# Two latent projections and a gate projection moved ahead of transpositions, and split projections that start on the high halves of their weights

## The reference

```
h = x @ w_in                       # split into a_q a_k a_v a_z | b_cq b_ckv b_kr b_z | c_q c_k c_v c_z
ya = moba_attention(a_q, a_k, a_v) * silu(a_z)      # with 256 tokens: causal softmax with ALiBi, 8 heads
cq, ckv = rmsnorm(b_cq), rmsnorm(b_ckv)             # the latents, up-projected for 8 heads
yb = mla_attention(cq @ w_uq, ckv @ w_ukv, rope) * silu(b_z)
yc = rmsnorm(diff_attention(c_q, c_k, c_v)) * silu(c_z)   # difference of two softmaxes, 4 heads
g  = sigmoid(x @ w_m + b_m)
out = (ga * (ya @ w_a) + gb * (yb @ w_b) + gc * (yc @ w_c)) @ w_o
r = ALPHA * x + out
r = r + sigmoid(r @ w_pg) * (p @ w_p)
return layernorm(r)
```

## Time and profile before

| | us |
|---|---|
| runs: median of 3 (lowest to highest) | 2129.71 (2129.71 to 2130.98) |
| the profiled execution | 2128.94 |
| its span | 2127.1 |
| PE busy | 2095.6 (99%) |
| DVE, ACT, POOL busy | 1412.5, 1297.7, 653.9 |

### The profile page before, as it was taken

One profiled execution on the slowest core, in us unless ns is written; L12 is line 12 of the kernel. 1 busy time (PEld: TensorE's weight loads), 2 busy tenths in 40 slices (PEclk: granted clock), 3 DMA queues, 4 the chain that ended last, 5 costly groups with the idle time before them and its releaser, 6 DMA issues.

```text
span 2127.1 us, 33542 instructions
## 1 busy us (share of the span) xinstructions
PE 2095.6 (99%) x13315; PEld 1865.4 (88%) x13315; DVE 1412.5 (66%) x1431; ACT 1297.7 (61%) x1427; POOL 653.9 (31%) x316
## 2 busy tenths in 40 slices
PE   9999999999999999999999999999999999999998
PEld 8979999988999898999998888888888888888887
DVE  1455223345422684323777989999999999999997
ACT  4556445455544544444545777777777777777776
POOL 5726885726787203888201000000000000000000
PEclk9999999999999999999999999999999999999999
DMA  7434564625455334556447999999999999999995
GB/s 245 137 111 150 176 196 149 189 70 164 151 194 179 121 100 149 191 194 197 141 140 230 382 377 332 376 357 366 363 351 371 362 369 346 364 356 370 367 365 202
DMA packets 307633, 529.06 MB, mean 249 GB/s; under 512 B 11842, under 2 KB 152802, under 8 KB 307520
## 3 DMA queue, kind: packets, MB, share of 16 engines
q1 hardware_dynamic: 306496, 525.92, 70.9%
q0 software_dynamic: 736, 1.00, 0.2%
q10 hardware_dynamic: 288, 0.52, 0.1%
HBM read 525.84 MB, written 1.05 MB: 248 GB/s over the span
## 4 chain that ended last, share of the span: by engine, by line
PE 84%; POOL 7%; DVE 3%; ACT 3%; issue 2%; DMA 1%; POOLq 0%; SPq 0%; DVEq 0%; ACTq 0%
PE bank L718 82%; POOL weights_low L3020 7%; PE bank L1474 1%; DVE qb L2288 1%; ACT sc L1619 1%; DMA ring<-in_w_in_dram 1%; ACT weights_high L1622 1%; DVE sc L2296 0%; DMA ring<-in_w_ple_dram 0%; DVE sc L2288 0%; PE bank L906 0%; PE bank L729 0%; DVE nmax L2323 0%; DVE h L2296 0%; ACT expert_weights_high L1622 0%
## 5 line engine op out<-in xcount | busy, mean ns | idle before, releaser
L2288 DVE TENSOR_TENSOR expert_weights_low<-ring_experts,expert_weights_high 128x2048 fp32r<-128x2048 f32 x336 | 764.7, 2289 | 72.4 <-ACT expert_weights_high L1622 72.4
L1622 ACT ACTIVATE expert_weights_high<-ring_experts 128x2048 fp32r<-128x2048 f32 x336 | 646.4, 1924 | 166.5 <-PE bank L718 162.1
L3020 POOL TENSOR_TENSOR weights_low<-ring,weights_high 128x1024 fp32r<-128x1024 f32 x252 | 616.7, 2470 | 344.5 <-ACT weights_high L1622 344.4
L1622 ACT ACTIVATE weights_high<-ring 128x1024 fp32r<-128x1024 f32 x294 | 303.7, 1056 | 327.1 <-PE bank L718 283.3
L718 PE MATMUL bank<-x_high,weights_high 128*128 128x256 f32 x1024 | 242.7, 280 | 1.3 <-POOL weights_low L3020 1.3
L718 PE MATMUL bank<-x_high,weights_low 128*128 128x256 f32 x1024 | 239.7, 277 | 0.0
L718 PEld LDWEIGHTS bank<-x_high,weights_high 128*128 128x128 f32 x1024 | 192.5, 188 | 2.8 <-DVE zs L2296 1.8
L718 PEld LDWEIGHTS bank<-x_high,weights_low 128*128 128x128 f32 x1024 | 192.5, 188 | 0.6 <-issue 0.5
L718 PE MATMUL bank<-expert_weights_high,gathered_high 128*128 128x512 f32 x456 | 180.7, 396 | 0.3 <-DVE gathered_low L2296 0.3
L718 PE MATMUL bank<-expert_weights_high,gathered_low 128*128 128x512 f32 x456 | 177.8, 390 | 0.0
L718 PE MATMUL bank<-expert_weights_high,gathered_high_b 128*128 128x512 f32 x448 | 177.5, 396 | 0.0
(11 more groups left out here) (335 smaller groups left out, 3739.2 us busy)
## 6 DMA issues: line engine op xcount, KB each, us to landing
ring_experts<-in_moe_w_gate_dram SPq DMA_DIRECT2D x112, 1024.0 KB, 6.3
ring_experts<-in_moe_w_up_dram SPq DMA_DIRECT2D x112, 1024.0 KB, 6.0
ring_experts<-in_moe_w_down_dram SPq DMA_DIRECT2D x112, 1024.0 KB, 5.7
ring<-in_w_in_dram SPq DMA_DIRECT2D x62, 1024.0 KB, 5.4
ring<-in_w_merge_dram SPq DMA_DIRECT2D x24, 1024.0 KB, 5.2
ring<-in_w_out_dram SPq DMA_DIRECT2D x14, 1024.0 KB, 5.0
ring<-in_ffn_w_gate_dram SPq DMA_DIRECT2D x11, 1024.0 KB, 5.4
ring<-in_ffn_w_up_dram SPq DMA_DIRECT2D x11, 1024.0 KB, 5.4
```

What stands on the lines that cost most here:

```text
L1622: return nc.scalar.activation(dst, src, ACT.Copy, scale=scale)
L2288: return nc.vector.tensor_tensor(dst, x, z, op)
L3020: nc.gpsimd.tensor_tensor(half_of(wlo[:, q_slot, :], t, width), half_of(ring[:, slot, :], t, width), half_of(whi[:, q_slot, :], t, width). ...
```

## The change

Three things. First, in `ORDER1`, in both layers of the first stack: `mc0` goes ahead of `("B", 1)`, `mc1` ahead of `("V", 1)` and so ahead of `("A", 2)`, and `mg2` ahead of `("B", 5)`. ACT's list follows: `take_turned(1)` comes behind `after("mc0")` and `latent(0)`, `take_y(1)` behind `latent(1)`, and `merge_gate(2)` ahead of `take_turned(5)`. Second, `split_project_first` waits for the high halves of its weights alone, does four inner tiles with them, then waits for the low halves, does the four tiles with those, and goes on with the other four in the same way; its low inputs come last, as before. Third, `cz0` gets a function of its own, which for each half does high x high and high x low first and the low weights last. No matmul, copy or transfer is added or taken away.

```diff
-    ("dv0", "a"), ("dv1", "a"), ("B", 1), ("mc0", "a"), ("V", 1), ("A", 2),
-    ("mc1", "a"), ("mc2", "a"), ("B", 2), ("ms", "a"), ("az0", "v"), ("V", 2), ("A", 3),
+    ("dv0", "a"), ("dv1", "a"), ("mc0", "a"), ("B", 1), ("mc1", "a"), ("V", 1), ("A", 2),
+    ("mc2", "a"), ("B", 2), ("ms", "a"), ("az0", "v"), ("V", 2), ("A", 3),
...
-    ("mg0", "a"), ("mg1", "a"), ("B", 5), ("mg2", "a"), ("mg3", "a"), ("V", 5),
+    ("mg0", "a"), ("mg1", "a"), ("mg2", "a"), ("B", 5), ("mg3", "a"), ("V", 5),
...
+            def split_project_low_last(b, slot, lo_at, x, count):
+                wh, wl = (w[:, slot, :].rearrange("p (k n) -> p k n", n=S) for w in (whi, wlo))
+                for t in range(2):
+                    cols = slice(t * P, (t + 1) * P)
+                    pe.wait_ge(hi_done.h, lo_at + t)
+                    for part in range(2):
+                        for kk in range(DT):
+                            mm(views(b)[:, t, :], wh[:, kk, cols], x[part][:, kk, :], part == 0 and kk == 0, False)
+                    pe.wait_ge(lo_done.h, lo_at + t)
+                    for kk in range(DT):
+                        ins = mm(views(b)[:, t, :], wl[:, kk, cols], x[0][:, kk, :], False, kk == DT - 1)
+                    ins.then_inc((used if t == 0 else count).h, 1)
...
             def split_project_first(b, slot, lo_at, x, count, wait_high, wait_low, settled=False):
-                pe.wait_ge(lo_done.h, lo_at + 1)
-                for kk in range(DT):
-                    if kk % 2 == 0:
-                        wait_high(kk // 2)
-                    if settled and kk == 0:
-                        settle(b, slot, xh)
-                    for t in range(2):
-                        cols = slice(t * P, (t + 1) * P)
-                        mm(views(b)[:, t, :], wh[:, kk, cols], x[0][:, kk, :], kk == 0 and t == 0, False, share=True)
-                        mm(views(b)[:, t, :], wl[:, kk, cols], x[0][:, kk, :], False, False, share=True)
+                pe.wait_ge(hi_done.h, lo_at + 1)
+                for k0 in (0, 4):
+                    for kk in range(k0, k0 + 4):
+                        if kk % 2 == 0:
+                            wait_high(kk // 2)
+                        if settled and kk == 0:
+                            settle(b, slot, xh)
+                        for t in range(2):
+                            mm(views(b)[:, t, :], wh[:, kk, t * P:(t + 1) * P], x[0][:, kk, :],
+                               kk == 0 and t == 0, False, share=True)
+                    if k0 == 0:
+                        pe.wait_ge(lo_done.h, lo_at + 1)
+                    for kk in range(k0, k0 + 4):
+                        for t in range(2):
+                            mm(views(b)[:, t, :], wl[:, kk, t * P:(t + 1) * P], x[0][:, kk, :], False, False, share=True)
...
+                        elif name == "cz0":
+                            split_project_low_last(begin(name), *take_split(name))
...
-                take_turned(1)
...
                 after("mc0")
+                latent(0)
+                take_turned(1)
+                latent(1)
                 take_y(1)
-                latent(0)
                 exps(2)
-                latent(1)
...
                 merge_gate(1)
+                merge_gate(2)
                 take_turned(5)
                 branch_high(2, 2)
-                merge_gate(2)
                 merge_gate(3)
```

## The result

| | before | changed |
|---|---|---|
| median of 13 runs each, us (lowest to highest) | 2130.01 (2127.74 to 2133.35) | 2135.18 (2132.08 to 2139.9) |
| the profiled execution | 2128.94 | 2132.21 |

The ratio of the times is 1.0024, with a 95% interval of 1.0017 to 1.0031: the change makes the kernel slower by a quarter of a per cent, 5.2 us. The prediction was 2135.1.

A forecast was written before the change was run, and what follows sets the result against it. PE was taken to bound the kernel, so only its idle stretches count. 2 x (2.9 - 0.7 - 0.88 - 0.4) + 0.8 = +2.6, plus 2.8 for the clock, +5.4: median 2135.1 us, 8-in-10 range 2131.5 to 2137.8.

The forecast's parts named there:

- Batch 1: Transpositions to scores of batch 2: PE's waits for sc (0.8) and y go, V starts 0.2 late, scores take 2.05.
- The new wait at batch 2: Before batch 2's transpositions: mc2's 7.1 can't cover the 11.26 chain, PE idles 4.2; +2.9 a layer including batch 1's gain.
- mg2: Moved ahead of batch 5's transpositions, it covers PE's wait of 0.55 + 0.2: -0.7 us a layer, bounds -0.9 and 0.
- ou0: Its start with high weights removes PE's wait of 0.65 + 0.2: -0.88 us a layer, bounds -0.95 and -0.4.
- cz0: Low weights wanted 1.9 later, its POOL wait goes but cz1 waits for the rest: -0.4 us a layer, bounds -0.9 and 0.
- Five starts: High-weight starts: aq0 and pg0 win nothing; gg twice and the feed-forward's first gate cost +0.27 each, +0.8 in all.
- three waits of 0.2 for `h_high`: Sign in PE's timeline: waits behind the fourth matmul in gg, twice, and the feed-forward's first gate, 0.2 us each.
- The clock: Behind batch 2's wait in each layer, TensorE's clock falls to 0.50: +1.4 us a layer, bounds 0 and 2.8.
- The bound of 2.8: Upper bound of the clock's cost behind batch 2's wait: two low-clock stretches in a row, 2.8 us a layer.
- the clock that holds: Rival: behind batch 2's wait the clock holds or falls once, +2.6 or +4.0, 2132.3 to 2133.7 us; chance 0.25.
- The term of the moved latents: mc0 and mc1 moved, batches 1 and 2: +2.9 us a layer without the clock, bounds +2.4 and +3.5.
- the three gains together: At batch 5 (mg2), ou0 and cz0: waits shortened or removed, -0.7, -0.88 and -0.4 us a layer.

The follow-up runs named there:

- the kernel with mc put back: The changed kernel with mc0 and mc1 back where they stood in table and ScalarE's order, the other changes kept; 2126.83 us, ratio 0.9975.
- both filled ones: The changed kernel with 16 or 8 matmuls of zeros between mc2 and batch 2's transpositions; 16: 2132.15 us, ratio 1.0006; 8: executed once, idle 2.29 us.
- the filled kernel: The changed kernel with 16 matmuls of zeros between mc2 and batch 2's transpositions in both layers; 2132.15 us, ratio 1.0006.

## Why the prediction was right, point by point

All terms are per layer where not said otherwise, from intervals between the same two instructions in two traces, so that a shift from earlier doesn't count.

- **Batch 1.** The recorded sum has `mc2` start at 106.84 against 107.55, 0.7 earlier; counted from V of batch 0 it started 1.24 earlier in layer 1 (107.45 - 76.98 = 30.47 against 107.55 - 75.84 = 31.71), and 1.1 earlier on average over both layers of two profiles of each kernel (30.51 against 31.62). The size that was off is the scores of batch 2. They took 107.45 - 105.84 = 1.61 and not 2.05, against 101.97 - 99.55 = 2.42 before (`mc1` starts at 101.97): the wait for `y` had cost 0.8, four times its bracket of 0.21, and not 0.4 (in the second profile of the kernel before 0.6, with no bracket at all). I took row lengths there, which reach past the next start, where only starts can be subtracted. The start of `mc0` came out by luck. I put it at 90.6, where the last row ends, but 0.8 of waiting ahead of 91.13 leave 90.33; and `mc0` waited for its first low half, 0.15 in the bracket and 0.3 from start to start, where I had looked only at the second. The two errors cancel. `("V", 1)` did not wait in this profile: it starts 1.00 after the last row of `mc1`, as before (97.05 and 98.05). In the second profile of the changed kernel it starts 1.12 after (103.10 and 104.22), about half of the foretold 0.2.
- **The new wait at batch 2.** Foretold: idle 4.2, transpositions 11.3 behind the scores, -0.55 at `ms`. Measured: 4.12, 118.86 - 107.45 = 11.41 from the start of `mc2` against 7.11 (+4.30), and -0.50 at `ms`. The rule to add 0.2 to a bracket held here. With batch 1, +2.56 in layer 1, and +2.7 with the average of batch 1, for the foretold +2.9.
- **mg2.** Foretold -0.7, measured -0.54 to -0.55. The wait of 0.55 + 0.2 is all gone, but `mg2` itself became slower by 0.11 a half, as its two pairs of rows below show. The term's size missed that.
- **ou0.** Foretold -0.88; -0.81 and -0.83.
- **cz0.** Foretold -0.4, half of it given back in `cz1`; measured -0.49, with the wait for POOL at the place named. In the changed kernel's first profile that wait is too short for the list of waits: the half starts 0.37 after the last matmul (188.46) where 0.12 is usual. A longer interval, from V of batch 3 to V of batch 4, takes in the 96 matmuls ahead of `cz0`, whose pace trades against this wait. It is 28.42 to 28.48 in all sixteen layers with the new order; with the old one it is 28.97 to 28.99 in seven of ten, and 28.57 to 28.59 in the three that had the slower pace ahead of `cz0` and the faster one in it. So the gain is 0.5 mostly and 0.1 at times.
- **Five starts.** In the profile of the kernel with mc put back, the first twelve steps of `gg` are 148.4 ns on average against 124.1 before at the same pace: 12 x 0.0243 = 0.29 for one pair, the foretold 0.27. Three such, +0.9. A line through all thirteen profiles (last section) gives +0.9 too. Of the three waits of 0.2 for `h_high` that were to show it none has a bracket here: the fifth matmul of this `gg` starts 0.30 after the fourth. (In the second profile of the changed kernel and in both filled ones the first `gg` does have a wait there, of 0.35; why is open.) Where the gate's matmuls go at the low clock, 0.21 apart, as in the changed kernel's first profile, there is no gap behind the fourth at all.
- **The clock.** Foretold +1.4 a layer. Measured from the start of the transpositions of batch 2 to V of batch 2. Filled with zeros it is 8.53. `az0` lies in this, and goes 0.2 faster at the faster of two paces (last section), so against 8.33 in such cases. In the changed kernel it is 128.88 - 118.86 = 10.02, +1.7; in its second layer 471.08 - 461.24 = 9.84, +1.5; in its second profile +1.3 and +1.7; and +2.5 where two stretches followed each other. The bound of 2.8 was near. A fall that starts while PE is still idle costs less behind it: +1.3 is where it came 0.64 before the transpositions. The runs of the filled kernel agree: 4.3 for two layers, with an uncertainty of some 2.

The sum by these terms: 2 x (2.56 - 0.54 - 0.82 - 0.49) + 0.9 = +2.3 (foretold 2.6), and +3.0 to 3.2 for the clock (foretold 2.8): +5.4. The runs gave +5.2. A check that needs no single term: from V of batch 0 to V of batch 5 a layer takes 144.15 in the changed kernel and 141.24 before (both layers of two profiles each), +2.9; with `ou0` and the five starts 2 x (2.9 - 0.82) + 0.9 = +5.1. Of the rivals, the clock that holds is what the filling made, and there the kernel is 0.9 above the kernel before (-0.6 to +3.2), where that rival had +2.6.

So the mechanism was right: each wait, each gain and both falls stand where they were foretold. That the median was met within 0.1 us is luck. The term of the moved latents was 0.2 to 0.3 a layer too dear, the three gains together 0.1 too large and the clock 0.1 to 0.2 too cheap, and these offset each other; the runs of one kernel spread over 5.6 and 7.8 us here.

The Trainium skill (TensorE: Matmul & The Clock Gate, "Why this matters for your kernels") warns against idle gaps between bursts of matmuls, as one brings the clock back to half. Here the clock fell at all six waits of 4.1, as the prediction read from it. For idleness as short as the 2.3 and 2.64 of these kernels the page gives no rule: there it fell in one of two and in 8 of 13.

## What to carry to other kernels

Before work is moved ahead of one wait, subtract it from the cover of the next: here 0.8 was won at the one and 4.3 lost at the other, because 12.6 of cover over a chain of 11.3 became 7.1, where half an operation was enough to close the short wait. The price of a long wait is also the slow clock behind it, and where the wait can't be closed, work whose result is thrown away can be cheaper than idleness, as it was here. Count in starts, never in row lengths, and read the whole list of the engine that answers: the wait for `y` hung on a weight's landing that stood ahead of it in ScalarE's list.

## What the runs showed of the hardware that was not expected

**Two paces of the same matmul at full clock.** Runs of split matmuls of 256 columns go at about 113.3 ns from start to start or at 117.8, and mostly keep it for as long as nothing interrupts them (1071 matmuls in a row in layers 1 and 2 of the changed kernel). An interruption can be slight: behind the feed-forward's first gate in the first profile of before the pace goes from 117.8 to 113.3 with no step above 122. `mg2`'s two rows of low inputs, before and in the changed kernel:

```profile
208.00 1.07 PE L718 MATMUL bank<-x_low,weights_high 128*128 128x256 f32 x8
210.72 1.07 PE L718 MATMUL bank<-x_low,weights_high 128*128 128x256 f32 x8
```

```profile
210.54 1.10 PE L718 MATMUL bank<-x_low,weights_high 128*128 128x256 f32 x8
213.37 1.11 PE L718 MATMUL bank<-x_low,weights_high 128*128 128x256 f32 x8
```

24 matmuls apart, 2.72 and 2.83. At some places every profile has the same pace: slow in `dv0`, `dv1`, `mg0` and `mg1`, fast behind the transpositions of batch 5. So an operation that is moved takes the pace of the run that it joins. At others it differs between two executions of one kernel (the first 288 matmuls: 113.3 in the first profile of before, 117.8 in the second, 1.3 us, of which 0.7 came back as a wait for POOL at 39.88), as large as a term of this study. The granted clock is 1.00 in both. What sets it was not found.

**Falls of the clock are in part chance.** From the last norm of layer 2 on the number of low stretches went from 0 to 6 over thirteen profiles with nearly the same work there. The time goes with it. From the squares for that norm (686.93 in the first profile of before) to the end:

| low stretches | 0 | 1 | 2 | 3 | 4 | 5 | 6 |
|---|---|---|---|---|---|---|---|
| starts as before, us | 1436.4 | 1438.0 | 1440.2, 1437.7 | 1440.2 | 1440.3 | 1442.3, 1441.8 | |
| new starts in `gg` and the gate, us | | | 1438.6 | 1441.1, 1441.4 | 1441.9 | | 1444.4 |

A straight line through the thirteen has 1.1 us for each stretch and 0.9 for the new starts. So several us of the 4 to 8 by which the runs of one kernel spread can be the falls. That they cause it is not shown, since no run here sets their number.
